# Fourier transform of the first pair by one radix-2 step over tokens and half of the frequencies, mirrored outputs from plus and minus mixing products

## The reference

```python
def fourier_mix(u, w_f):                       # u: (b, n, 256), n = 512 tokens, or 256 of the context
    ug = u.reshape(b, n, 4, 64).astype(float32)
    f = jnp.fft.fft2(ug, axes=(1, 3), norm='ortho').real
    return jnp.einsum('bngc,gcd->bngd', f, w_f).reshape(b, n, 256)

q, k, v, ga, uf, gf, zc, bc, cc, gc = split_cols(hx @ w_in, PROJ_SIZES)
f = fourier_mix(uf, w_fourier)
h = concatenate([a * silu(ga), f * silu(gf), s * silu(gc)])
```

## Time and profile before

| | |
|---|---|
| median of 3 runs | 1957.68 us (1957.17 to 1959.28) |
| profiled execution, span | 1955.8 us |
| PE busy | 1925.2 us, 98% |
| ACT busy | 829.7 us, 42% |
| DVE busy | 807.3 us, 41% |
| POOL busy | 704.9 us, 36% |

### The profile page before, as it was taken

How to read it: one execution, slowest core, us unless ns; L and a number is a source line. 1 busy time by engine, 2 the same in 40 slices (tenths; PEclk the granted TensorE clock), 3 DMA queues, 4 the chain that set the end, 5 groups by cost and what they waited for, 6 DMA issues and landing times.

```text
span 1955.8 us, 26905 instructions
## 1 busy us (share of the span) xinstructions
PE 1925.2 (98%) x10454; PEld 1633.5 (84%) x10454; DVE 807.3 (41%) x1827; ACT 829.7 (42%) x1582; POOL 704.9 (36%) x553
## 2 busy tenths in 40 slices
PE   8999999999999999999999999999999999999997
PEld 4898889878889888888888888888888898888886
DVE  3665557543556445576511110027367551111003
ACT  3321268365237556686232322115478432323222
POOL 0523312125440344311444445445321344444442
PEclk9999999999999999999999999999999999999999
DMA  9544311022340124211333333323420223333321
GB/s 282 163 163 162 119 65 45 19 57 87 108 146 6 57 68 131 88 55 44 87 86 105 89 108 108 108 78 95 122 81 23 66 77 105 99 94 100 128 88 44
DMA packets 198261, 183.72 MB, mean 94 GB/s; under 512 B 31702, under 2 KB 166220, under 8 KB 198136
## 3 DMA queue, kind: packets, MB, share of 16 engines
q1 hardware_dynamic: 192104, 170.67, 28.6%
q10 hardware_dynamic: 6032, 11.33, 1.9%
HBM read 179.86 MB, written 5.40 MB: 95 GB/s over the span
## 4 chain that ended last, share of the span: by engine, by line
PE 90%; ACT 3%; DVE 3%; issue 2%; POOL 2%; DMA 0%; SPq 0%; ACTq 0%; DVEq 0%
PE ps L1341 24%; PE ps L1343 24%; PE ps L1342 24%; PE ps L1938 3%; PE ps L1434 3%; PE ps L1855 3%; PE ps L1401 2%; POOL w_lo L733 2%; PE ps L1956 2%; PE ps L1420 2%; PE ps L1464 1%; ACT w_hi L788 1%; PE ps L1379 1%; PE ps L1362 1%; PE ps L1658 0%
## 5 line engine op out<-in xcount | busy, mean ns | idle before, releaser
L733 POOL TENSOR_TENSOR w_lo<-raw,w_hi 128x512 fp32r<-128x512 f32 (+1 forms) x518 | 679.9, 1343 | 1152.4 <-ACT w_hi L788 1152.3
L788 ACT ACTIVATE w_hi<-raw 128x1024 fp32r<-128x1024 f32 (+2 forms) x261 | 258.5, 1036 | 251.5 <-PE ps L1343 190.8
L1341 PE MATMUL ps<-g_hi,w_lo 128*128 128x512 f32 (+1 forms) x928 | 348.4, 375 | 1.4 <-POOL w_lo L733 1.4
L1342 PE MATMUL ps<-g_lo,w_hi 128*128 128x512 f32 (+1 forms) x928 | 347.5, 374 | 0.0
L1343 PE MATMUL ps<-g_hi,w_hi 128*128 128x512 f32 (+1 forms) x928 | 347.5, 374 | 0.0
L1341 PEld LDWEIGHTS ps<-g_hi,w_lo 128*128 128x128 f32 x928 | 174.7, 188 | 33.7 <-issue 1.7
L1343 PEld LDWEIGHTS ps<-g_hi,w_hi 128*128 128x128 f32 x928 | 174.7, 188 | 31.4
L1342 PEld LDWEIGHTS ps<-g_lo,w_hi 128*128 128x128 f32 x928 | 174.7, 188 | 30.9
L2659 DVE TENSOR_TENSOR tmp_f<-ps,tmp_f 128x512 f32<-128x512 f32 x44 | 30.4, 691 | 370.7 <-PE ps L1343 370.7
L1341 PE MATMUL ps<-h_hi,w_lo 128*128 128x512 f32 (+1 forms) x496 | 180.2, 363 | 3.3 <-DVE h_lo L2076 2.3
L1343 PE MATMUL ps<-h_hi,w_hi 128*128 128x512 f32 (+1 forms) x496 | 174.6, 352 | 0.0
(11 more groups left out here) (292 smaller groups left out, 3472.6 us busy)
## 6 DMA issues: line engine op xcount, KB each, us to landing
raw<-in_w_in SPq DMA_DIRECT2D x30, 1024.0 KB, 5.3
raw<-in_w_mod SPq DMA_DIRECT2D x24, 1024.0 KB, 6.1
raw<-in_w_gate SPq DMA_DIRECT2D x44, 512.0 KB, 4.0
raw<-in_w_up SPq DMA_DIRECT2D x44, 512.0 KB, 5.2
raw<-in_w_down SPq DMA_DIRECT2D x22, 1024.0 KB, 4.8
raw<-in_w_out SPq DMA_DIRECT2D x8, 1024.0 KB, 5.0
strips<-bias_rows ACTq DMA_DIRECT2D x18, 256.0 KB, 3.2
raw<-in_w_in SPq DMA_DIRECT2D x16, 256.0 KB, 4.5
```

The source lines that it names most:

```text
L733: pool.tensor_tensor(w_lo[:, i % SPLIT, a:e], raw_of(what)[:, a:e], w_hi[:, i % SPLIT, a:e].bitcast(F32), ALU.subtract).then_inc(s_tile_lo ...
L788: act.activation(w_hi[:, i % SPLIT, a:b], raw_of(what)[:, a:b], ACT.Copy).then_inc(s_tile_hi.sem, s_tile_hi.nth((what, n)))
L1341: pe.matmul(o, lhs[1], rhs[0], start=first, stop=False)
L1342: pe.matmul(o, lhs[0], rhs[1], start=False, stop=False)
```

## The change

The token transform takes one radix-2 step: with x1 the first and x2 the second 256 tokens, x1 + x2 gives the even and x1 - x2 the odd frequencies. Since the input is real, C is even and S is odd in the frequency, so only half of the frequencies are transformed, with C and S side by side in one matmul of 260 or 256 columns; the result at a frequency is A C + B S, at the mirrored one A C - B S. The mixing products are made once with +B and once with -B (a negated copy of it, put into `wf`), and DVE writes the gates for even and odd, rising and falling frequencies with steps of two and minus two.

The constants become one tile of 1552 columns (1032 in the second layer) in place of three (two) tiles of 2048. "uf" is folded on the way: ACT copies token tiles 0 and 1 to `fold_x`, which lies in the space of `cz`; DVE adds and subtracts token tiles 2 and 3; ACT makes the high parts of the folded values, DVE the low parts. The core of the diff:

```diff
 # ACT
-                for g in range(nt // 2):
-                    act.wait_ge(s_mm.sem, s_mm.at((l, ("uf",), g, 0)))
-                    act.activation(uf_hi[:, 2 * g:2 * g + 2, :]..., ps[:, (7, 6, 5)[g], :], ACT.Copy)
+                act.wait_ge(s_mm.sem, s_mm.at((l, ("uf",), 0, 0)))
+                act.activation(fold_x[:, 0, :], ps[:, 7, :], ACT.Copy).then_inc(s_fold_in.sem, s_fold_in.nth(l))
                 split_next()
+                if both:
+                    act.activation(uf_hi[:, 4:6, :]..., ps[:, 5, :], ACT.Copy)
                 for part, n in ((0, XT), (1, CT)):
                     act.activation(v1[...], ps[:, part, 0:n * P], ACT.Copy)
+                for g in range(2):
+                    act.wait_ge(s_folded.sem, s_folded.at((l, g)))
+                    act.activation(uf_hi[:, 2 * g:2 * g + 2, :]..., fold_x[:, 1 + g, :], ACT.Copy)
                 for what, func, dst in (("gf", ACT.Silu, gf), ("zc", ACT.Copy, cz), ("bc", ACT.Copy, cb)):
+                    if what == "zc":
+                        act.wait_ge(s_uf_lo.sem, s_uf_lo.at((l, 1)))
...
-                split_next()
                 k_hi(0)
-                k_hi(1)
...
+                for g in range(2):
+                    for c in range(2):
+                        four_part(g, c)
                 if both:
                     four_ctx(0)
-                    exp1(l, units, 2)
                     four_ctx(1)
+                k_hi(1)
+                for i in range(EARLY1):
+                    exp1(l, units, i)
 # PE
-                    emptied[b] = s_uf_lo.after((l, g))
+                    emptied[b] = (s_fold_in.after(l), s_folded.after((l, 1)), s_uf_lo.after((l, 2)))[g]
...
+                def waves(b, t0, a, n):
+                    pe.wait_ge(*emptied[b])
+                    for k in range(2):
+                        o = a + 2 * n * k
+                        m = mm3(ps[:, b, 0:2 * n], both_parts(U, lambda r: r[:, t0 + k, P * (b % 2):P * (b % 2) + P]),
+                                both_parts(w, lambda r: r[:, o:o + 2 * n]), k == 0, k == 1)
+                for g in range(2):
+                    for c in range(2):
+                        waves(2 * g + c, 2 * g, 4 * EVEN * g, (EVEN, ODD)[g])
+                if both:
+                    for c in range(2):
+                        waves(4 + c, XT, 4 * (EVEN + ODD), EVEN)
+                def mix_waves(c, part):
+                    pe.matmul(ps[:, b, 0:less], wf_m[:, 0, c, :], src[:, c, 0, 0:less], start=True, stop=False)
+                    pe.matmul(ps[:, b, 0:less], wf[:, l, c, :], src[:, c, 1, 0:less], start=False, stop=True)
+                    pe.matmul(ps[:, b, less:less + n], wf_m[:, 0, c, :], src[:, c, 0, 0:n], start=True, stop=False)
+                    pe.matmul(ps[:, b, less:less + n], wf_m[:, 1, c, :], src[:, c, 1, 0:n], start=False, stop=True)
+                mix_waves(0, 0)
+                score1(l, units, 0)
+                mix_waves(1, 0)
+                score1(l, units, 1)
+                for c in range(2):
+                    if both:
+                        mix_waves(c, 1)
+                    score1(l, units, 2 + c)
 # DVE
+                V.tensor_scalar(wf[:, l, :, :], wf_m[:, 1, :, :], -1.0, None, ALU.mult)
...
+                V.tensor_tensor(fold_x[:, 1, :], ps[:, 6, :], fold_x[:, 0, :], ALU.add)
+                V.tensor_tensor(fold_x[:, 2, :], fold_x[:, 0, :], ps[:, 6, :], ALU.subtract)
+                weigh((4, 13)[l])
+                if both:
+                    uf_low(2, ps[:, 5, :])
+                for g in range(2):
+                    uf_low(g, fold_x[:, 1 + g, :])
...
+                        for to, o in ((falling, 0), (rising, up)):
+                            V.tensor_tensor(to, ps[:, b, o:o + 2 * ODD]...[:, :, 0:last], to, ALU.mult)
+                        gate_some(c, b, (last, last + 1, 1), gf[:, c, half + 1:half + 2])
+                        gate_some(c, b, (up + last, up + WAVES - 1, ODD), gf[:, c, half - 1:half + 1])
+                        gate_some(c, b, (up + WAVES - 1, up + WAVES, 1), gf[:, c, 0:1])
```

More of the change, by code:

```diff
@@ L44 @@
 QC = HD + ROPE
+EVEN, ODD = SEQ // 4 + 2, SEQ // 4
+WAVES = 2 * ODD + 1
 class Signal:
@@ L69, in after, with _half_transforms @@
         return self.sem, self.at(key)
+def _half_transforms(f):
+    row = np.arange(SEQ // 2)
+    folded = [*range(1, SEQ // 4), SEQ // 4, 0, 0]
+    even = [2 * m for m in folded]
+    odd = [2 * m + 1 for m in range(SEQ // 4)]
+    cols = []
+    for n, freqs in ((SEQ, even), (SEQ, odd), (CTX, folded)):
+        for k in range(2):
+            t = np.outer(row[P * k:P * k + P], freqs) % n * (2 * np.pi / n)
+            cols += [np.cos(t) / np.sqrt(n), np.sin(t) / np.sqrt(n)]
+    return np.ascontiguousarray(np.concatenate(cols, 1).astype(f))
 def _constants():
@@ L385, in cols, with width @@
             return w[:, a:b].rearrange("(k p) c -> p k c", p=P)
+        def width(what):
+            if what[1] == "up":
+                return 2 * C_HEADS * (QC + HD)
+            if what[1] == "dft":
+                return 4 * (EVEN + ODD) + (4 * EVEN if what[0] < DEPTH - 1 else 0)
+            return {"c": 4 * 416, "av": 4 * 384}.get(what[1], TILE)
         def mod_tile(l, j):
@@ L404, in mix_tiles @@
                 proj(("ga", j), [(0, 768 + 256 * j, 256)])
[L405 to L412, removed]
+            n = width((l, "dft"))
+            t.append(((l, "dft"), [(lambda r: r[:, 0:n], I["dft"][:, 0:n])], True))
             return t
@@ L1703, in _ @@
-                pe.wait_ge(s_wf_m.sem, s_wf_m.at(l))
-                for part in range(parts):
-                    for c in range(2):
-                        b, n, a = (6 + c, SEQ, 0) if part == 0 else (2 + c, CTX, SEQ)
-                        pe.wait_ge(s_four_out.sem, s_four_out.at((l, 1, c if part == 0 else "ctx")))
-                        pe.wait_ge(*emptied[b])
-                        emptied[b] = s_side.after((l, c))
-                        for i in range(2):
-                            m = pe.matmul(ps[:, b, 0:n], wf_m[:, i, c, :], four[:, i, c, a:a + n], start=i == 0, stop=i == 1)
-                        m.then_inc(s_fmix.sem, s_fmix.nth((l, c, part)))
-                        if not both:
-                            score1(l, units, 2 + c)
+                pe.wait_ge(s_uf_lo.sem, s_uf_lo.at((l, 1)))
@@ new lines, in _ @@
+                left((l, "dft"))
+                pe.wait_ge(s_wf_m.sem, s_wf_m.at(l))
+                pe.wait_ge(s_wf_neg.sem, s_wf_neg.at(l))
+                def mix_waves(c, part):
+                    b, n, src = (6 + c, WAVES, four) if part == 0 else (2 + c, EVEN - 1, four_c)
+                    less = n - 2
+                    pe.wait_ge(s_four_out.sem, s_four_out.at((l, 1, c) if part == 0 else (l, c, "ctx")))
+                    pe.wait_ge(*emptied[b])
+                    emptied[b] = s_side.after((l, c))
+                    pe.matmul(ps[:, b, 0:less], wf_m[:, 0, c, :], src[:, c, 0, 0:less], start=True, stop=False)
+                    pe.matmul(ps[:, b, 0:less], wf[:, l, c, :], src[:, c, 1, 0:less], start=False, stop=True)
+                    pe.matmul(ps[:, b, less:less + n], wf_m[:, 0, c, :], src[:, c, 0, 0:n], start=True, stop=False)
+                    pe.matmul(ps[:, b, less:less + n], wf_m[:, 1, c, :], src[:, c, 1, 0:n], start=False,
+                              stop=True).then_inc(s_fmix.sem, s_fmix.nth((l, c, part)))
```

117 lines of the change are left out of this document (52 added, 65 removed).

## The result

The changed kernel takes **1963.78 us** (median of 6 runs, 1961.71 to 1966.58) against 1957.62 for the kernel before: a ratio of 1.0029, interval 1.0019 to 1.0039. It is slower by 6.2 us, more than the 3.9 that the prediction takes for the limit of what can be told from no change; 1955.7 was predicted, with a range that ended at 1962.0. Nearly all the mechanisms of the sum are in the trace, most at nearly the predicted sizes. What was not in the sum is TensorE's clock at the start of attention and a second wait behind the stall.

A forecast was written before the change was run, and what follows sets the result against it. TensorE, busy 98% of the span, was taken as the bound: 1955.8 - 6.6 - 6.2 + 8.8 + 1.5 + 0.5 = 1953.8 us; the median lies 1.9 above the span, giving 1955.7, range 1948.5 to 1962.

The forecast's parts named there:

- Transform products, first layer: Transforms to first attention output product, first layer: fewer columns on PE, gain 6.6 us, ends 4.0 and 9.5.
- The gates on DVE: First layer's attention start: five gate instructions per 128 channels, 1.2 us a wide set, 0.65 a context set, delay first output.
- Transform products, second layer: Transforms to first attention transpose, second layer: gain 6.2 us instead of 8.0 because ACT comes late; ends 5.2 and 7.0.
- The stall: Second layer, before PE's third rotation product: folded "uf" parts wait behind the "zc" split and v; 8.8 us, ends 5.9, 9.8.
- The first layer's copy of the chain: Fold to first rotation, first layer: rotation ends at 138.3, PE wants the bank at 144.00; hidden, 5.7 us to spare.
- The rivals of a short stall and of none: Second layer: short, 5.9 instead of 10.3 us with clock kept, 1951.3, chance 0.20; none, 1945.4, chance 0.06.
- What follows the stall: Second layer, after the stall: PE resumes at half clock for some 3.5 us, costing 1.5 us (0 to 2.5).
- The sentence that the next rotation product finds its bank free: Second layer, behind the stall: bank freed at about 522, when PE arrives, so no second wait.
- The pause at the start of the span: Basis for the clock's price: after 2.82 us idle, PE resumed at 7.01; clock averaged 0.64 from 10 to 11 us.
- The "bc" tile, first layer: First layer: "bc" load issued later, usable at 164.2, wanted at 165.0; cover 0.8 us, cost 0.5 us, 0 to 3.
- The rival on the slower side: First layer: bias rows hold the "bc" tile to 169, costing 6.5 us instead of 0.5; 1961.7, chance 0.12.

The follow-up runs named there:

- the filled stall: Changed kernel with unread matmuls on ones in PE's gaps, 33 before the second layer's third rotation product, others at both layers' attention starts: 1955.22 us.
- one with the stall filled: Changed kernel with only the 33 unread matmuls on ones before the second layer's third rotation product: 1965.16 us median, 1963.56 in the second profile's run.
- the kernel before with the delay: Kernel before with twelve small DVE operations ahead of the first layer's context gates: median 1960.89 us; seven runs 1959.6 to 1961.4, three 1965.0 to 1966.3.

## Why the prediction was wrong

- **Transform products, first layer: right.** Predicted 6.6 us to the first output product, measured 7.2. The gates on DVE do bind, a little cheaper than estimated: 0.93 us for a wide set (1.2 predicted), 0.46 for a context set (0.65). DVE's timeline, channel half 0, without the context's:

```profile
270.34 0.73 DVE L2416 TENSOR_TENSOR gf<-ps,gf 128x254 f32<-128x254 f32 x2
270.99 0.28 DVE L2406 TENSOR_TENSOR gf<-ps,gf 128x1 f32<-128x1 f32 x3
```

- **Transform products, second layer: right, somewhat large.** Predicted 6.2, measured 5.4 where the clock stays (E to end 1374.7 against 1380.1), 4.9 in the changed kernel, where it falls for 3.4 us.
- **The stall: right in each link.** Predicted 8.8 us, measured 7.9. The two low parts took 2.53 us together (2.8 predicted), the cosine and sum operations 1.04 and 1.64 (1.4 each). The first layer's copy of the chain was hidden, as predicted. The rivals of a short stall and of none are out.
- **What follows the stall: mis-sized.** The sentence that the next rotation product finds its bank free was wrong at full clock (1.7 us), and the clock costs some 2.3 us, not 1.5. Together 4.0 where 1.5 stood, above the end of 2.5. That the clock's share came out so near is luck: PE worked at half clock for 8.3 us, not 3.5, and the second wait hid part of the price. The pause at the start of the span could not give that price. PE's matmuls on ones took 0.23 us a record there already ahead of the pause (row below, kernel before), where the same matmul took 0.11 in the filled stall (66 records in 7.53 us) at full clock. So PE was at half pace before it paused, though the profile gives 1.00 as the granted clock of these first microseconds.

```profile
0.99 3.20 PE L1447 MATMUL ps<-ones 128*128 128x128 f32 x14 [0.99 <-POOL ones L724]
```

- **The "bc" tile, first layer: in its bounds.** A to B grew by 0.9 us in one profile of the changed kernel and by nothing in two, and by 0.6 in one with the stall filled; 0.5 was predicted. The rival on the slower side, which put the upper end of the range, did not happen.
- **The step that failed: the clock was priced behind the one long stall alone.** The working itself said that the gates make PE wait at the start of the first layer's attention (a gain of 9.5 us by the columns, of 6.6 with the gates) and entered these 2.9 us as gain not made. It did not ask what waits in close order do to the clock. The fall behind them cost 6.3 us in the profiled execution and 5.0 in the timed runs, most of the 7.2 gained at the stage. With it and the second wait the sum on the span reads 1955.8 - 7.2 + 6.3 (first layer: products, clock) - 5.4 + 0.5 (second layer: products, clock) + 8.1 + 1.7 + 2.3 (stall, second wait, clock) + 0.9 ("bc") = 1963.0, and 1.6 for the late start of that execution make its 1964.6.

The Trainium skill ("TensorE: Matmul & The Clock Gate", HAM oscillation — how this bites in real kernels) describes a kernel in which each wait for a transfer sends the clock back to half rate, so that the loss is paid again and again. The stall here agrees: within 7.9 us of waiting the clock fell to 0.50, and PE worked at it for 8.3 us afterwards. The traces add that much shorter waits, for DVE and ACT, in close order are enough: behind those of 0.41, 0.92 and 0.93 us it was 0.50 for 6.8 or 13.7 us.

## What to carry to other kernels

Work taken off the busiest engine uncovers the short waits that it covered, and on TensorE waits of under a microsecond in close order can cost more afterwards, through the clock, than by themselves (3.2 or 6.3 us against 2.3 here): add up the idle time that a shortened stage will have, and price the half clock behind it. Look for the instruction that is queued behind a late landing for no reason of its own (two copies here, 13 us); and a fall of the clock can hide a second wait, so that taking away the one shows the other.

## What the runs showed of the hardware

- The clock's fall is a matter of chance near the edge: the same gaps gave 6.8 or 13.7 us at 1.2 GHz in the first layer, 3.4 us or none in the second, and, by time and mean clock, none in seven runs of ten of the kernel before with the delay. It widens the spread of a kernel's times: 1961.7 to 1966.6 for the changed kernel, 1957.2 to 1959.3 for the one before, in the same comparison.
- Matmuls whose results nobody reads keep the clock at 2.4 GHz over a wait of 8 us; seven of them in two of the first layer's three gaps were worth 5 us.
- Writes with a step of two or minus two cost DVE nothing extra: one gate of each kind, of 254 values, took 0.73 us together, where a single 256-wide gate took 0.42.
